# RWKV's chunked scan over chunks of 64 tokens in place of 32, with one more doubling level within a chunk

## The chip, the cores and the metric

The kernel runs on one core of one Trainium2 chip, as one program. The metric is the device time of an execution in microseconds (us). Engines are named as in the profile: PE is TensorE's matrix multiply and PEld its weight load, DVE is VectorE, ACT is ScalarE, POOL is GpSimd, SP is SyncE, which issues most transfers.

## The reference

Two small networks run one behind the other on 256 tokens of width 1024, all in float32. The first has two layers of feed-forward halves around a Fourier mixer and a retention mixer. The second has two layers; each projects its input, runs three mixers side by side (RWKV-7, compressed and windowed attention, sliding-window attention), merges them, and ends in a mixture of 16384 small experts. The change touches only the RWKV mixer, which has 8 heads of width 64. Its core is a recurrence over tokens:

```python
def step(state, inp):
    r_t, w_t, k_t, v_t, kk_t, a_t = inp
    sa = jnp.einsum('bhij,bhj->bhi', state, -kk_t)
    state = (state * w_t[:, :, None, :] + sa[..., None] * (kk_t * a_t)[:, :, None, :]
             + v_t[..., None] * k_t[:, :, None, :])
    return state, jnp.einsum('bhij,bhj->bhi', state, r_t)
```

A group norm per head, a bonus term and a gate follow.

## The kernel before, in words

The program is a list of stages. Each stage has a method for each engine, and each engine runs its stages' methods in turn; the order of the work on an engine is thus written out by hand, and semaphores (`wait_ge`, `then_inc`) tie the engines together. Weights come as blocks of 1 MB into a ring of four (`load_block`, issued by SyncE as blocks are used up). For most products ScalarE rounds a block (L232), GpSimd takes the rest (L260), and TensorE makes three products of it (L244 to L246).

In each layer of the second network the order of stages is: norm, `ProjectIn`, `Attention`, `Rwkv`, `Merge`, and then projection and experts. `Attention` begins with the preparation of RWKV's operands (`prepare_pe`, `prepare_act`, `prepare_dve`, `prepare_pool`); on VectorE `prepare_dve` stands ahead of all of the attention's own work. It takes the running sum of the log decay within each chunk by doubling: for shifts 1, 2, 4, 8, 16 a copy (L1947) and a shifted addition (L1948) between two buffers, each with the chunk as the innermost dimension. Exponentials (L1884 to L1887) and products with them (L1970 to L1976, GpSimd's L2118 to L2124) give the decayed operands A, R, b, k and the ones decayed to the end of the chunk.

The `Rwkv` stage goes over two tiles of 128 tokens (t = 0, 1), all heads at a time. Per tile:

- TensorE transposes four operands (L1773), and makes the 128x128 matrices of key products (L1784); VectorE masks them to the lower triangle within each chunk (L2023).
- The inverse of (1 + lower triangle) is built by doubling, in `LEVELS` = 5 levels: from blocks of 1 to blocks of 32. A level takes, for two groups of four heads: a mask of the level (L2033), the product ct d (L1795), a copy to SBUF by ScalarE (L1912), two more products (L1812, L1813) and the subtraction from d and dt by VectorE (L2054, L2055). Level 0 needs only L1795, L2045 and L2046. The last level updates dt alone (L1813, L2055).
- Three products with the inverse (L1817, L1820, L1826), each kept by ScalarE (L1920, L1923, L1925), give w1 and w2.
- The scan goes over the tile's four chunks of 32 tokens. TensorE: w1 times state (L1842), state times R (L1845), the update from this chunk's 32 rows (L1848), then the next chunk's keys and values, also from 32 rows (`keys_values`, L1834). VectorE: decay the state (L2073), add w2 (L2075), add keys and values (L2080), add the update (L2084). The next L1842 waits for L2084.
- The output of the whole tile within its chunks (L1856, L1857), kept by ScalarE (L1931) and VectorE (L2091).

In tile t = 1 the group norm of tile 0 is placed between the levels. TensorE: `sums(0)` after level 0's products, `squares(0)` after level 2's, `bonus(0)` after level 3's (all L1752). VectorE: `centre(0)` behind level 1 (L1992), `spread(0)` behind level 3 (L1997), `finish(0)` behind level 4 (L2004 to L2013: a reciprocal, a product, four scalings, a product, a sum, a product). ScalarE: a square (L1897) and a square root (L1901). The tests that place them name the level by its number:

```python
                if t:
                    if lv == 1:
                        centre(0)
                    if lv == 3:
                        spread(0)
                    if lv == 4:
                        finish(0)
            dve.wait_ge(s["w2_kept"].sem, s["w2_kept"].at(t + 1))
```

In t = 1, once w2 is kept, ScalarE and GpSimd begin to round and split the attention's outputs and the `Merge` stage's first weights (L2174, L232, L2194, L260) beside the scan. After the second tile come its own group norm and the first products of `Merge`.

Of the kernel before, what the change touches and what calls it, by code (L numbers as in the profile page):

```python
# [37 lines left out]
DH = 64  # L38
GN_EPS = 64e-5
HEADS = 8  # L40
CH = 32
NCH = N // CH
CMP_LEN, CMP_STRIDE = 32, 16
NCMP = N // CMP_STRIDE - CMP_LEN // CMP_STRIDE + 1
NEG = -1e30
# [47 lines left out]
class Share:  # L93
# [3 lines left out]
    def at(self, k):  # L97

        return self.base + k
# [1100 lines left out]
B_OC = B_OB + 4 * N  # L1200
B_OA = B_OC + 4 * N
B_CST2 = B_OA + 4 * N
NCST2 = 2 * P + 5 * P + 2 * 16
B_BIAS = 23328
assert B_CST2 + NCST2 <= B_BIAS
B_WORK = B_BIAS + 16 * N
# [126 lines left out]
class Attention(Stage):  # L1333
# [14 lines left out]
    def __init__(self, chip, layer, tables):  # L1348
        super().__init__(chip)
        at, sig = chip.at, chip.signals  # L1350
        self.layer, self.tables = layer, tables
        self.p = at(B_P, 56, N)
        self.o = {self.WIN: at(B_OB, 4, N), self.SWA: at(B_OC, 4, N)}
        self.bias = at(B_BIAS, 16, N)
        self.cmask = at(B_CST2 + 7 * P, 2, 16)

        self.r = at(W_R, CMP_LEN, 2, 2, NCMP)
        n = B_U
        self.hid_rows = at(n, 2 * P)
        n += 2 * P  # L1360
        self.hid = at(n, 4, 2 * NCMP)
        n += 4 * 2 * NCMP
        self.kcm, self.vcm = at(n, 16), at(n + 16, P)
        n += 16 + P
        assert n + self.BUFS * 8 * 4 <= W_PEND
        self.stat = at(n, self.BUFS, 8, 4)
        self.sc = at(B_WORK, self.BUFS, 4, N)
        n = B_WORK + self.BUFS * 4 * N
        self.pt = at(n, 5, 4, P)
        self.pts = at(n + 20 * P, 2, 4, P)  # L1370
        u = len(self.units)
        self.blocks_ready = sig("cmp_blocks_ready", 1)
        self.hidden = sig("cmp_hidden", 1)
        self.hidden_turned = sig("cmp_hidden_turned", 1)
        self.hidden_kept = sig("cmp_hidden_kept", 1)
        self.compressed = sig("cmp_done", 1)
        self.cmp_kept = sig("cmp_kept", 1)
        self.scored = sig("scored", u)
        self.biased = sig("attn_biased", u)
        self.shifted = sig("shifted", u)  # L1380
        self.exped = sig("exped", u)
        self.scale_ready = sig("attn_scale_ready", u)
        self.weighted = sig("weighted", u)
        self.turned = sig("turned", u)
        self.turned_kept = sig("attn_turned_kept", u)
        self.summed = sig("summed", u // 2)
        self.sum_kept = sig("sum_kept", u // 2)
# [256 lines left out]
class Rwkv(Stage):  # L1644
# [7 lines left out]

    LEVELS = 5

    def __init__(self, chip, layer):
        super().__init__(chip)
# [86 lines left out]
    def pe(self, pe):  # L1745
# [21 lines left out]
        for t in range(NT):  # L1767
# [66 lines left out]
                    mm(ps[:, c % 2, i * P:(i + 1) * P], self.tok[rows_, 2, i, :], self.tok[rows_, 3, i, :], start=True, stop=True)  # L1834

            keys_values(0)
            for c in range(4):
                n = 4 * t + c
                rows_ = slice(c * CH, (c + 1) * CH)
                pe.wait_ge(s["s_kept"].sem, s["s_kept"].at(n + 1))  # L1840
                for i in range(4):
                    last = mm(ps[:, 4, i * P:(i + 1) * P], self.w1[:, i, :], self.state[:, i, :], start=True, stop=True)  # L1842
                last.then_inc(s["sa_done"].sem, 1)
                for i in range(4):
                    mm(ps[:, 5, i * P + c * CH:i * P + (c + 1) * CH], self.state[:, i, :], self.R[:, i, n * CH:(n + 1) * CH], start=True, stop=True)  # L1845
                pe.wait_ge(s["sa_kept"].sem, s["sa_kept"].at(n + 1))
                for i in range(4):
                    last = mm(ps[:, 2 + c % 2, i * P:(i + 1) * P], self.tok[rows_, 1, i, :], self.sa[rows_, i, :],  # L1848
                              start=True, stop=True)
                last.then_inc(s["s_done"].sem, 1)  # L1850
                if c < 3:
                    keys_values(c + 1)
            for e in range(2):
                for i in range(4):
# [83 lines left out]
    def prepare_dve(self, dve, link):  # L1938
        ps, z, s, v = self.chip.ps, self.z, self.s, self.nc.vector
        col = lambda name, i: columns(self.chip.vec, name, self.layer, 4)[:, i:i + 1]  # L1940
        two = lambda bank: ps[:, bank:bank + 2, :].rearrange("p b (i n) -> p (b i) n", n=N)
        dve.wait_ge(s["sig_w"].sem, s["sig_w"].at(1))
        c = [x.rearrange("p i (c n) -> p (i c) n", n=CH) for x in self.c]
        link(v.tensor_scalar(self.c[0], self.c[0], -math.exp(-0.5), None, ALU.mult))
        for n in range(5):
            of, to, d = c[n % 2], c[1 - n % 2], 1 << n
            v.tensor_copy(to[:, :, 0:d], of[:, :, 0:d])  # L1947
            last = v.tensor_tensor(to[:, :, d:CH], of[:, :, d:CH], of[:, :, 0:CH - d], ALU.add)  # L1948
            if n < 4:
                link(last)  # L1950
        last.then_inc(s["c_ready"].sem, 1)
        dve.wait_ge(s["c_ready"].sem, s["c_ready"].at(1))
        e2 = self.e[2].rearrange("p i (c n) -> p (i c) n", n=CH)
        v.tensor_tensor(e2, c[1][:, :, CH - 1:CH].broadcast_to([P, 4 * NCH, CH]), c[1], ALU.subtract).then_inc(s["end_in"].sem, 1)
        dve.wait_ge(s["sig_a"].sem, s["sig_a"].at(1))
        t3 = self.t3
        for i in range(4):
            last = v.tensor_scalar(t3[:, i, :], self.a[:, i, :], 1.0, col("k_a", i), ALU.subtract, ALU.mult)
        link(last)
        k = z[:, T_K:T_K + 4, :]  # L1960
        link(v.scalar_tensor_tensor(k, t3, 1.0, k, ALU.add, ALU.mult))
        v.tensor_tensor(self.a, self.a, self.kk, ALU.mult).then_inc(s["ak_ready"].sem, 1)
        dve.wait_ge(s["ak_ready"].sem, s["ak_ready"].at(1))
        dve.wait_ge(s["exps"].sem, s["exps"].at(1))
        dve.wait_ge(s["end_exp"].sem, s["end_exp"].at(1))
        e_in, e_inv, e_end = self.e
        split = lambda x: x.rearrange("p i (c n) -> p i c n", n=CH)
        for i in range(4):
            A, kk, e = (x[:, i, :].rearrange("p (c n) -> p c n", n=CH) for x in (self.A, self.kk, e_in))
            v.tensor_tensor(A[:, :, 1:CH], kk[:, :, 1:CH], e[:, :, 0:CH - 1], ALU.mult)  # L1970
            v.tensor_copy(A[:, :, 0:1], kk[:, :, 0:1])
        v.tensor_copy(self.pend, split(e_in)[:, :, :, CH - 1])
        v.tensor_tensor(self.b, self.a, e_inv, ALU.mult).then_inc(s["ab_ready"].sem, 1)
        dve.wait_ge(s["rk_raw"].sem, s["rk_raw"].at(1))
        v.tensor_tensor(self.R, self.R, e_in, ALU.mult)
        link(v.tensor_tensor(self.k, self.k, e_inv, ALU.mult))  # L1976
        dve.wait_ge(s["hats_ready"].sem, s["hats_ready"].at(1))

    def dve(self, dve, link):
# [35 lines left out]
        for t in range(NT):  # L2015
# [47 lines left out]
                    if lv == 4:  # L2063
                        finish(0)
            dve.wait_ge(s["w2_kept"].sem, s["w2_kept"].at(t + 1))
            for c_ in range(4):
                n = 4 * t + c_
                rows_ = slice(c_ * CH, (c_ + 1) * CH)
                halves = [slice(e * DH, (e + 1) * DH) for e in range(2)]
                decayed = [self.gn[0][half, :, 0:DH] for half in halves]  # L2070
                ends = [ps[half, :, :].rearrange("p b (i n) -> p b i n", n=P)[:, :, :, half] for half in halves]
                for e, half in enumerate(halves):
                    v.tensor_tensor(decayed[e], self.state[half, :, half], self.pend[half, :, n:n + 1].broadcast_to([DH, 4, DH]), ALU.mult)  # L2073
                dve.wait_ge(s["sa_done"].sem, s["sa_done"].at(n + 1))
                last = v.tensor_tensor(self.sa[rows_].rearrange("p i n -> p (i n)"), ps[rows_, 4, :],  # L2075
                                       self.w2[rows_].rearrange("p i n -> p (i n)"), ALU.add)
                last.then_inc(s["sa_kept"].sem, 1)
                dve.wait_ge(s["sa_kept"].sem, s["sa_kept"].at(n + 1))
                for e in range(2):
                    last = v.tensor_tensor(decayed[e], decayed[e], ends[e][:, c_ % 2], ALU.add)  # L2080
                link(last)
                dve.wait_ge(s["s_done"].sem, s["s_done"].at(n + 1))
                for e, half in enumerate(halves):
                    last = v.tensor_tensor(self.state[half, :, half], decayed[e], ends[e][:, 2 + c_ % 2], ALU.add)  # L2084
                last.then_inc(s["s_kept"].sem, 1)
                dve.wait_ge(s["s_kept"].sem, s["s_kept"].at(n + 2))
# [710 lines left out]
def second_constants():  # L2797
# [3 lines left out]
    s, t = p[:, None], p[None, :]  # L2801
    same = s // CH == t // CH
    parts = [same & (s <= t), same & (s < t)]
    for n in (1, 2, 4, 8, 16):
        parts.append((s // (2 * n) == t // (2 * n)) & (s % (2 * n) < n) & (t % (2 * n) >= n))
    end = np.arange(16) * CMP_STRIDE + CMP_LEN - 1
    seen = [np.where(end[None, :] <= (p + k * P)[:, None], 0.0, NEG) for k in range(NT)]
# [267 lines left out]
```

## Time and profile before

| | us |
|---|---|
| median of 3 runs | 4928.53 |
| lowest and highest | 4918.61, 4930.82 |
| the profiled execution: span from its first to its last instruction | 4928.1 |
| busy: PE, PEld | 4534.2, 4089.3 |
| busy: DVE, ACT, POOL | 1550.8, 1764.8, 2802.4 |

The profile is of one execution, and its span stands for that execution's own time: what lies around the span is not listed apart. It is 0.4 us below the median. Busy time is the time in which an engine works on instructions; TensorE's instructions overlap, so a busy TensorE is not one at its peak. The granted clock (PEclk) is the share of 2.4 GHz that TensorE was given in a stretch; it has two levels, 1.00 (2.4 GHz) and 0.50 (1.2 GHz), and a value between them is a mean over a stretch with both. In the trace one float32 product appears as two records.

### The profile page before, as it was taken

What the parts mean: (1) busy time and instruction counts of PE and PEld (TensorE: products, weight loads), DVE (VectorE), ACT (ScalarE), POOL (GpSimd) and SP (SyncE); (2) the same over time, 40 slices, a digit from 0 to 9 for tenths busy, and PEclk for the clock granted to TensorE, in tenths of its full rate; (3) what the DMA queues carried; (4) which work ended last, traced back from release to release, by engine and by line L of the source; (5) the groups of instructions that cost most, each with busy time, mean ns of one, the idle gap of its engine ahead of it and who ended that gap; (6) DMA issues with size and microseconds to landing.
All of it is one profiled execution on the core that took longest, in us unless ns stands there. A gap on an engine that the chain in (4) does not pass through costs nothing.

```text
span 4928.1 us, 72992 instructions
## 1 busy us (share of the span) xinstructions
PE 4534.2 (92%) x30090; PEld 4089.3 (83%) x30090; DVE 1550.8 (31%) x3001; ACT 1764.8 (36%) x2766; POOL 2802.4 (57%) x1354
## 2 busy tenths in 40 slices
PE   8999999999999898998867999999998866999999
PEld 5777777787878798967856999999977866999999
DVE  2211211121023331444577111112444668111112
ACT  3223322232233343441233444444441233444444
POOL 3443333444445376830467888887840467888887
PEclk9999999999999999978788999999987888999999
DMA  6624364222223144420130454545430130545554
GB/s 253 245 89 94 113 238 179 94 94 94 93 96 119 69 171 158 171 95 1 52 112 18 180 186 179 184 182 192 167 115 1 52 112 1 186 180 181 185 179 153
DMA packets 94372, 648.51 MB, mean 132 GB/s; under 512 B 9824, under 2 KB 16224, under 8 KB 16608
## 3 DMA queue, kind: packets, MB, share of 16 engines
q1 hardware_dynamic: 87120, 633.21, 35.2%
q10 hardware_dynamic: 7056, 12.49, 1.1%
q8 instruction: 147, 2.41, 0.2%
q14 instruction: 49, 0.40, 0.0%
HBM read 641.47 MB, written 4.19 MB: 131 GB/s over the span
## 4 chain that ended last, share of the span: by engine, by line
PE 85%; DVE 11%; ACT 2%; issue 1%; POOL 1%; DMA 1%; SPq 0%; DVEq 0%; ACTq 0%; POOLq 0%
PE ps L244 23%; PE ps L245 23%; PE ps L246 23%; PE ps L2551 3%; PE ps L399 1%; PE ps L1442 1%; PE ps L1473 1%; DVE arena L2108 1%; PE ps L1795 1%; POOL ring_rest L260 1%; PE ps L1842 1%; PE ps L1005 1%; DMA arena<-in_mod_weights 1%; PE ps L1454 1%; PE ps L1848 1%
## 5 line engine op out<-in xcount | busy, mean ns | idle before, releaser
L260 POOL TENSOR_TENSOR ring_rest<-ring,rounded 128x1024 fp32r<-128x1024 f32 x1032 | 2508.4, 2452 | 1594.1 <-ACT rounded L232 1324.9
L244 PE MATMUL ps<-part,rounded 128*128 128x256 f32 (+1 forms) x5760 | 1839.0, 319 | 82.0 <-DVE part L2216 22.4
L245 PE MATMUL ps<-part,rounded 128*128 128x256 f32 (+1 forms) x5760 | 1827.2, 317 | 0.0
L246 PE MATMUL ps<-part,ring_rest 128*128 128x256 f32 (+1 forms) x5760 | 1825.7, 317 | 0.0
L244 PEld LDWEIGHTS ps<-part,rounded 128*128 128x128 f32 x5760 | 1111.7, 193 | 184.7 <-issue 27.5
L246 PEld LDWEIGHTS ps<-part,ring_rest 128*128 128x128 f32 x5760 | 1111.0, 193 | 69.1
L245 PEld LDWEIGHTS ps<-part,rounded 128*128 128x128 f32 x5760 | 1112.1, 193 | 66.9
L232 ACT ACTIVATE rounded<-ring 128x1024 fp32r<-128x1024 f32 x528 | 528.4, 1050 | 739.2 <-PE ps L246 731.3
L2673 ACT ACTIVATE rounded<-ring 128x1024 fp32r<-128x1024 f32 x504 | 531.4, 1054 | 376.3 <-DMA ring<-in_weights 369.2
L244 PE MATMUL ps<-x_parts,rounded 128*128 128x256 f32 x2304 | 654.9, 284 | 4.8 <-DVE x_parts L577 3.4
L245 PE MATMUL ps<-x_parts,rounded 128*128 128x256 f32 x2304 | 653.3, 284 | 0.0
L246 PE MATMUL ps<-x_parts,ring_rest 128*128 128x256 f32 x2304 | 653.3, 284 | 0.0
L244 PEld LDWEIGHTS ps<-x_parts,rounded 128*128 128x128 f32 x2304 | 443.7, 193 | 5.6 <-DVE x_parts L577 3.8
L245 PEld LDWEIGHTS ps<-x_parts,rounded 128*128 128x128 f32 x2304 | 443.8, 193 | 0.0
L246 PEld LDWEIGHTS ps<-x_parts,ring_rest 128*128 128x128 f32 x2304 | 443.6, 193 | 0.0
L2703 DVE TENSOR_TENSOR ps<-ps,arena 128x256 f32<-128x256 f32 x256 | 160.1, 625 | 677.0 <-ACT ps L2652 677.0
L2706 DVE TENSOR_TENSOR part<-ps,part 128x256 fp32r<-128x256 f32 x256 | 108.8, 425 | 523.0 <-ACT part L2658 523.0
L677 ACT ACTIVATE arena<-ps 128x512 f32<-128x512 f32 (+1 forms) x88 | 47.9, 544 | 617.8 <-PE ps L246 617.8
L2652 ACT ACTIVATE ps<-ps 128x256 f32<-128x256 f32 x256 | 94.2, 368 | 410.6 <-PE ps L246 410.6
L691 DVE TENSOR_TENSOR part<-ps,arena 128x512 f32<-128x512 f32 (+1 forms) x88 | 55.0, 625 | 556.9 <-ACT arena L677 556.9
L763 DVE SCALAR_TENSOR_TENSOR x<-ps,mods,x 128x256 f32<-128x256 f32 x80 | 35.8, 480 | 506.9 <-PE ps L246 506.9
L2194 POOL TENSOR_TENSOR part<-arena,part 128x1024 fp32r<-128x1024 f32 x6 | 14.2, 2369 | 290.8 <-ACT part L2174 290.8
(333 smaller groups left out, 4275.1 us busy)
## 6 DMA issues: line engine op xcount, KB each, us to landing
ring<-in_weights SPq DMA_DIRECT2D x528, 1024.0 KB, 4.8
arena<-in_mod_weights SPq DMA_DIRECT2D x72, 1024.0 KB, 7.8
arena<-bias_scratch ACTq DMA_DIRECT2D x2, 2048.0 KB, 9.1
bias_scratch<-arena ACTq DMA_DIRECT2D x1, 3072.0 KB, 32.2
x<-in_x SPq DMA_DIRECT2D x1, 2048.0 KB, 9.7
arena<-in_keys ACTq DMA_DIRECT2D x2, 1024.0 KB, 4.7
arena<-in_cst SPq DMA_DIRECT2D x1, 1216.0 KB, 28.2
arena<-in_expo ACTq DMA_DIRECT2D x1, 1024.0 KB, 4.9
```

The lines of the kernel that those rows point to most:

```text
L232: self.nc.scalar.activation(c.rounded[:, s % ROUNDED, half], c.ring[:, slot, half], ACT.Copy)\
L244: mm(out, w[0], a[0], start=start, stop=False)
L245: mm(out, w[0], a[1], start=False, stop=False)
L246: return mm(out, w[1], a[0], start=False, stop=stop)
L260: eng.tensor_tensor(c.ring_rest[:, slot, half], c.ring[:, slot, half], c.rounded[:, (self.s0 + r) % ROUNDED, half].bitcast(F32), ALU.subtr ...
L399: last = mm(c.ps[g * self.TILE:(g + 1) * self.TILE, self.BANK + n % 2, 0:width], self.cond[:, k, :], w[:, at:at + width], start=k == 0, st ...
L691: v.tensor_tensor(self.h[:, j, :], self.chip.ps[:, 2 * (j % 2) + 1, 0:self.t], self.silu[:, j % 2, :], ALU.mult)\
L2551: last = self.nc.tensor.matmul(self.chip.ps[:, n % self.BANKS, i * P:(i + 1) * P], self.hot[:, n % self.BUFS, 0, i], self.hot[:, n % self. ...
L2652: copy(self.hidden(r), c.ps[:, r % 2, 0:N], ACT.Gelu).then_inc(self.gelu_ready.sem, 1)
L2673: self.nc.scalar.activation(c.rounded[:, (self.s0 + r) % ROUNDED, half], c.ring[:, f % RING, half], ACT.Copy)\
L2703: v.tensor_tensor(gelu, gelu, self.gates[:, :, bass.ds(b, 1)].rearrange("p t a -> p (t a)"), ALU.mult)\
L2706: v.tensor_tensor(self.parts[1][:, r % 2, :], gelu, self.parts[0].bitcast(F32)[:, r % 2, :], ALU.subtract)\
```

## The change

A chunk gets 64 tokens, so a tile has two chunks (`CPT`) and the whole sequence four. The doubling within a chunk gets a sixth level, from blocks of 32 to blocks of 64, with a mask of its own in the constants, and the running sum gets a sixth shift. For the running sum to end in the same buffer, its first scaling writes to the other one. The placement of `centre`, `spread` and `finish` by level number is not touched.

```diff
-CH = 32
+CH = 64
 NCH = N // CH
+CPT = P // CH
+LEVELS = 6
+assert 1 << LEVELS == CH
...
-NCST2 = 2 * P + 5 * P + 2 * 16
+NCST2 = 2 * P + LEVELS * P + 2 * 16
...
-        self.cmask = at(B_CST2 + 7 * P, 2, 16)
+        self.cmask = at(B_CST2 + (2 + LEVELS) * P, 2, 16)
...
-    LEVELS = 5
+    LEVELS = LEVELS
...
-            for c in range(4):
-                n = 4 * t + c
+            for c in range(CPT):
+                n = CPT * t + c
...
-                if c < 3:
+                if c < CPT - 1:
                     keys_values(c + 1)
...
-        link(v.tensor_scalar(self.c[0], self.c[0], -math.exp(-0.5), None, ALU.mult))
-        for n in range(5):
-            of, to, d = c[n % 2], c[1 - n % 2], 1 << n
+        first = (LEVELS + 1) % 2
+        link(v.tensor_scalar(self.c[first], self.c[0], -math.exp(-0.5), None, ALU.mult))
+        for n in range(LEVELS):
+            of, to, d = c[(first + n) % 2], c[(first + n + 1) % 2], 1 << n
             v.tensor_copy(to[:, :, 0:d], of[:, :, 0:d])
             last = v.tensor_tensor(to[:, :, d:CH], of[:, :, d:CH], of[:, :, 0:CH - d], ALU.add)
-            if n < 4:
+            if n < LEVELS - 1:
                 link(last)
...
-            for c_ in range(4):
-                n = 4 * t + c_
+            for c_ in range(CPT):
+                n = CPT * t + c_
...
-    for n in (1, 2, 4, 8, 16):
+    for n in (1 << i for i in range(LEVELS)):
         parts.append((s // (2 * n) == t // (2 * n)) & (s % (2 * n) < n) & (t % (2 * n) >= n))
```

## Rows read from the trace of the kernel before

**Rows 1.** The page: busy time by engine, and the chain that ended last by engine.

```profile
PE 4534.2 (92%) x30090; PEld 4089.3 (83%) x30090; DVE 1550.8 (31%) x3001; ACT 1764.8 (36%) x2766; POOL 2802.4 (57%) x1354
...
PE 85%; DVE 11%; ACT 2%; issue 1%; POOL 1%; DMA 1%; SPq 0%; DVEq 0%; ACTq 0%; POOLq 0%
```

**Rows 2.** Windows, RWKV tile t = 0: length, busy by engine, granted clock, DMA share, GB/s.

```profile
2235.00:2322.00 87.00, 75.33 (x494) 71.18 (x496) 42.08 (x75) 12.46 (x22) 0.00 (x0) 0.78 0.00 1
```

**Rows 3.** Chain of waits in time, one chunk step: start, us, what.

```profile
2287.06 1.36 PE ps L1848 x5
2289.07 1.02 PE ps L1834 x5
```

**Rows 4.** Timeline of chunk steps, t = 0: start, us, engine, line, operation.

```profile
2283.44 2.08 PE L1842 MATMUL ps<-arena 128*128 128x128 f32 x8
...
2285.31 1.75 PE L1845 MATMUL ps<-arena 128*128 128x32 f32 x8
2285.55 0.68 DVE L2075 TENSOR_TENSOR arena<-ps,arena 32x512 f32<-32x512 f32 x1 [3.27 <-PE ps L1842]
...
2289.17 0.85 DVE L2084 TENSOR_TENSOR arena<-arena,ps 64x256 f32<-64x256 f32 x2 [2.05 <-PE ps L1848]
...
2290.08 2.07 PE L1842 MATMUL ps<-arena 128*128 128x128 f32 x8
...
2306.89 2.07 PE L1848 MATMUL ps<-arena 32*128 32x128 f32 x8
```

**Rows 5.** Timeline of doubling levels, t = 0, second head group and last level.

```profile
2263.23 1.13 PE L1795 MATMUL ps<-arena 128*128 128x128 f32 x8 [0.71 <-DVE arena L2055]
...
2269.54 1.13 PE L1795 MATMUL ps<-arena 128*128 128x128 f32 x8 [0.71 <-DVE arena L2055]
...
2271.67 0.69 DVE L2055 TENSOR_TENSOR arena<-arena,ps 128x512 f32<-128x512 f32 x1 [2.28 <-PE ps L1813]
```

**Rows 6.** Windows around levels, scan, output products and attention (columns as rows 2).

```profile
2243.00:2247.00 4.00, 2.43 (x12) 2.46 (x13) 2.40 (x5) 0.00 (x0) 0.00 (x0) 0.71 0.00 0
2247.00:2251.00 4.00, 2.79 (x17) 2.34 (x17) 3.93 (x7) 0.60 (x1) 0.00 (x0) 0.87 0.00 0
...
2263.00:2267.00 4.00, 3.77 (x34) 3.80 (x35) 1.59 (x4) 0.75 (x2) 0.00 (x0) 1.00 0.00 0
...
2283.00:2287.00 4.00, 4.00 (x20) 3.71 (x19) 1.40 (x3) 0.00 (x0) 0.00 (x0) 0.50 0.00 0
...
2183.00:2189.00 6.00, 6.00 (x16) 4.18 (x16) 2.86 (x5) 2.12 (x10) 0.28 (x1) 0.50 0.00 0
...
2309.00:2314.60 5.60, 5.60 (x32) 5.44 (x32) 0.84 (x2) 0.00 (x0) 0.00 (x0) 0.65 0.00 0
```

**Rows 7.** Timeline of TensorE: attention scores, first level, w1 and w2 products.

```profile
2181.74 3.78 PE L1442 MATMUL ps<-arena 64*128 64x256 f32 x8
...
2244.57 3.65 PE L1795 MATMUL ps<-arena 128*128 128x128 f32 x16 [3.16 <-DVE arena L2033]
...
2273.36 1.83 PE L1817 MATMUL ps<-arena 128*128 128x128 f32 x14 [0.85 <-DVE arena L2055]
...
2277.84 2.85 PE L1826 MATMUL ps<-arena 128*128 128x64 f32 x16 [0.69 <-ACT arena L1923]
```

**Rows 8.** Timeline of VectorE, t = 1: finish(0) and the first chunk steps.

```profile
2358.61 3.35 DVE L2004 RECIPROCAL arena<-arena 128x512 f32<-128x512 f32 x1
...
2365.32 0.69 DVE L2013 TENSOR_TENSOR arena<-arena 128x512 f32<-128x512 f32 x1
2366.54 0.85 DVE L2073 TENSOR_TENSOR arena<-arena 64x256 f32<-64x256 f32 x2 [0.53 <-ACT arena L1925]
...
2375.24 4.35 DVE L2073 TENSOR_TENSOR arena<-arena 64x256 f32<-64x256 f32 x2
```

**Rows 9.** Chain of waits in time, the running sum in prepare_dve.

```profile
2126.01 0.20 DVE arena L1947
...
2127.34 0.20 DVE arena L1947
```

## The prediction

> **What bounds the kernel now.** First the page's busy shares and its chain of waits: TensorE is busy 92% of the span and is 85% of the chain that ended last [rows 1]. The change touches only the RWKV part of the two layers of the second network: two token tiles (t = 0 and t = 1, 128 tokens each) in each layer, four tiles in all, 87 us for the first and about as much for each of the others [rows 2]. So a few per cent of the span are in play, and what a step is worth has to be read from the timeline.
>
> Second the chain through one chunk step of the scan (t = 0). It stays on TensorE: the products with w1 (L1842), those with the state (L1845), those that give the new state (L1848), the next chunk's keys and values (L1834), then the next step [rows 3]. The timeline gives the pitch: the step's first product starts at 2283.44 and again at 2290.08, thus 6.64 us [rows 4]. VectorE's work (L2075, L2084) lies just beside it: L2084 runs from 2289.17 to 2290.02, 0.06 us before the next L1842, so both engines bound the step nearly equally [rows 4].
>
> Third the doubling levels: the second head group's L1795 starts at 2263.23 and again at 2269.54, a pitch of 6.31 us, at a granted clock of 1.00 (2.4 GHz) [rows 5, 6]. The scan runs at 0.50 (1.2 GHz) although TensorE is busy 4.00 of each 4.00 us [rows 6]. That is the heart of the trade: a level costs nearly what a chunk step costs.
>
> **What the change does, part by part.** *Fewer chunk steps.* Two steps go from each tile, whole ones, since the last stays the last: 2 x 6.64 = 13.28 us less per tile. The two that stay get larger operands. L1848 and L1834 contract over 64 rows in place of 32: 8 records of 32 rows take 2.07 us (L1848) and 8 of 128 rows 2.08 (L1842) [rows 4], so 64 rows cost the same. L1845 gets 64 columns for 32; 8 records take 1.75 us with 32 columns and 2.08 us with 128 (L1842) [rows 4], so at most 0.33 us more per step, 2.6 us over the 8 steps left; I take nothing, because 16 records of 64 columns (L1826) take 2.85 us, less for each than the 1.75 for 8 [rows 4, 7]. L2075 reads 64 partitions for 32 with the same 512 elements in each: 0.68 us, while L2055 with 128 partitions takes 0.69 [rows 4, 5]; nothing. The two pend columns fewer per tile are a copy of a few elements.
>
> The 4 L1848 products and the next chunk's 4 L1834 products fill the chain from 2287.06 to 2290.08, 3.0 us, where 16 records at 0.22 us (8 L1845 from 2285.31 to 2287.06) would need 3.5 [rows 3, 4]: they overlap a little at their border because they sit on different row strips. With 64 rows they still do (0:64 and 64:128). If they did not: 0.5 us per whole step, 2.0 us over four tiles. The Trainium skill speaks against this change here (TensorEngine Tiling, When to Use Tiling): a contraction of 32 allows 4x row tiling, one of 64 only 2x. By that rule the removed concurrency would raise each step's price; the rows show that the products of one chunk, all on one strip, were never concurrent, so the sum leaves it out.
>
> *One more level.* + 6.31 us per tile, read at the full clock. Its masks (L2033) go one level ahead and are in that pitch. It is inserted before the last one, which is shorter on VectorE in old and new alike.
>
> *Where finish(0) stands.* In t = 1 VectorE does the previous tile's group norm: centre after level 1, spread after 3, finish after level 4. Level 4 was the last, so finish(0) ran beside TensorE's w1, x2 and w2 products: from 2358.61 to 2366.01, 7.40 us, and VectorE had nothing to do until 2366.54 anyway [rows 8]. Its cost was nothing, and its cover was the wait for w2. The diff leaves the test at level 4, now the last but one; finish(0) stands ahead of the last level's L2055. At t = 0 VectorE is idle for 2.28 us, until 2271.67, between the L2055 of these two levels [rows 5]. So 7.40 - 2.28 = 5.1 us stick out on the path, once per layer. Queued behind it on VectorE are the last L2055s; w1, x2 and w2 on TensorE wait for them, and then ScalarE and the scan. The root that finish needs is there: ScalarE's square root follows its level-4 copies and its table load, and TensorE's bonus sums come at level 3, so neither adds a wait. The pause on TensorE grows from 0.85 us [rows 7] to 6.0.
>
> *The clock behind that pause.* After the 3.16 us pause ahead of the first level, L1795 ran its 16 records in 3.65 us [rows 7]; the clock was 0.71 and 0.87 in those two stretches of 4 us, which is 2.3 and 1.0 us at half clock [rows 6]. L1817 has 16 records of the same kind and took 1.83 for 14 at full clock [rows 7]. So 3.3 us at half clock cost 1.7 us; if the low clock holds on for L1820 it is as much again, and 0.5 for L1826, partly slow already: + 1.7 to + 3.9. I take 2.0 per layer, nearest to the one episode that rows 6 show.
>
> *The prefix sum in prepare_dve.* The list of shifts becomes 1 to 32 over 16 groups of 64, in place of 1 to 16 over 32 groups of 32. A copy of n x d elements and an addition of the rest: shifts 2 to 32 of the new have the sizes of 1 to 16 of the old, and the new first one (copy of 16, sum of 1008) costs about what the old first did, from 2126.01 to 2127.34: + 1.3 us. This lies on the chain [rows 9], so + 1.3 per layer. The other exponentials and products keep their sizes.
>
> *The constants* grow by 128 columns (one more mask) in a load issued long before: nothing.
>
> *POOL's splitting of weights in t = 1* makes a copy group of VectorE (L2073) last 4.35 us for 0.85 in the second chunk step [rows 8]. It starts after w2 as before, two steps remain and so does this stall: nothing either way.
>
> **Sum.** t = 0: - 13.3 + 6.3 = - 7.0. t = 1: - 13.3 + 6.3 + 5.1 + 2.0 = + 0.1. Prefix sum + 1.3. One layer - 5.6 us, two layers - 11.2 us. Against the profiled execution's span of 4928.1 us this is 4916.9; that execution is 0.4 us below the median of the runs shown (4928.53), so 4917.3, and I predict 4917 us. About 0.3%, 15 us, is what a measurement of this kernel can tell from no change; the three runs lie 12 us apart. The forecast is just within it.
>
> **The rivals.** *Full clock in the scan* (chance 0.12). The scan's matmuls fill a quarter of the array's rows (L1848, L1834) or of the columns (L1845), and the change doubles each. For: the full 128x128 work of L1856 and L1857 that follows the scan in t = 0 brings the clock back (0.65 from 2309 to 2314.6) [rows 6]. Against: the attention's 64-row, 256-column products stand at 0.50 too (L1442, and the stretch from 2183 to 2189) [rows 6, 7], and those are as full as the new ones. Then a step becomes, L1842 and L1848 at half their 2.08 and 2.07, L2075 0.7, L2084 0.9 and an estimated 0.3 of hand-overs = 4.0 in place of 6.6. Two steps per tile, 2.6 each, and about 2 for L1856 and L1857, which now are half slow: 7 per tile, 28 in all: 4889 us; half of it if only two tiles get there, 4903. The Trainium skill (TensorE: Matmul & The Clock Gate, Part 1) has it that sustained activity of TensorE releases the throttle. By that rule the scan of before, busy 4.00 of 4.00 us, would run at full clock; the trace disagrees, at 0.50, so the rule alone gives this rival no more.
>
> *The late finish is hidden after all* (0.10). If the pause does not cost the 2.0, and finish overlaps more than I see, both layers get up to 2 x 7.1 = 14.2 back: 4903 us. Against: VectorE executes in program order, and 7.40 us do not fit in 2.28.
>
> *The trade turns round* (0.10): the added level runs at the low clock. Its place is the last level of each tile; its price: 16 L1795 records and 32 of L1812/L1813 at 0.22 us are 10.5 us in place of 6.3. For it: the first level of t = 0 began at 0.71 after a pause [rows 6], and in t = 1 group-norm work stands between the levels. In all four tiles, with finish and the 3.9 of its pause: t = 0 - 2.8, t = 1 + 6.2, prefix + 1.3: + 4.7 per layer, + 9 in all, 4937 us, slower than before. It decides where the added level exceeds its 6.3 by 2.8 us on average over the four tiles, since that is the forecast's 11.2. Against: at t = 0 the levels from the third on stand at 1.00. To be slower by more than 15 us, other levels would have to slow down too.
>
> *Forecast* (0.68): 4917, own range 4909 to 4926 (the bounds of L1845 and the clock terms, and up to 1.2 us per tile for where in L1856/L1857 the clock comes back).
>
> **Chances and range.** Faster by over 0.3% (below 4913.7): the full clock 0.12, most of the hidden finish 0.07, and 0.13 from the forecast's lower end: 0.32. Slower by over 0.3%: 0.03. Within: 0.65. The range 4902 to 4927 leaves out the full clock in all tiles and most of the turned trade.
>
> **What would show it.** Right: two L1842 pitches of 6.6 us per tile fewer; L1795 for six levels, with a pitch of 6.3 us at t = 0; the RWKV tile of t = 0 shorter by 7 us and that of t = 1 by nearly nothing; in t = 1, L2004 ahead of the last two L2055, and TensorE waiting about 6 us ahead of L1817 for L2055; L1817 above 3 us; six pairs of L1947/L1948, 1.3 us more. Wrong: a granted clock of 1.00 between L1834 and L1848, a step longer than 7 us at t = 0, or L1817 following the last level within 1 us in t = 1.

## The result and the profile after

| | before | after | ratio, 95% interval |
|---|---|---|---|
| first measurement, 4 runs each: median us | 4923.84 | 4895.21 | 0.9947 [0.9930, 0.9963] |
| second measurement, 9 and 5 runs | 4926.55 | 4894.61 | 0.9933 [0.9920, 0.9947] |

The change makes the kernel 29 to 32 us faster. I had said 11 us, with a range that ended at 4902, so the direction held and the size did not. The first profile of after is of an execution of 4900.47 us, the slowest of its four; a second profile (called `again` below) is of one of 4894.61 us, the median of its five.

The page of the first profile of after, busy time and chain by engine:

```profile
PE 4489.2 (92%) x30026; PEld 4049.4 (83%) x30026; DVE 1542.7 (31%) x2973; ACT 1770.5 (36%) x2774; POOL 2804.4 (57%) x1354
...
PE 84%; DVE 11%; ACT 2%; issue 1%; POOL 1%; DMA 1%; SPq 0%; DVEq 0%; ACTq 0%; POOLq 0%
```

Next to [rows 1], TensorE's busy time fell by 45 us. The trade explains some 30 of them: eight steps of 6.6 us, all busy, against four levels of 48 records at 0.12 us. The other 15 us are time that the trade does not account for; since a busy TensorE takes longer at the lower clock, they point to the granted clock, which the stretches below show.

The scan of tile t = 0 in layer 0 (timeline of after):

```profile
2282.38 2.07 PE L1845 MATMUL ps<-arena 128*128 128x128 f32 x8
2284.24 1.81 PE L1848 MATMUL ps<-arena 128*128 128x64 f32 x8
...
2289.07 2.08 PE L1845 MATMUL ps<-arena 128*128 128x128 f32 x8
...
2292.68 2.07 PE L1851 MATMUL ps<-arena 64*128 64x128 f32 x8
```

Line numbers are 3 higher than before at this place. Against [rows 4]: the pitch is 2289.07 - 2282.38 = 6.69 us (6.64 before), L1848 with 64 columns takes 1.81 us (1.75 with 32), and L1851 with 64 rows 2.07 (the same as with 32). Larger operands cost next to nothing, as costed.

The late finish(0) in tile t = 1 (timeline of `again`, VectorE, then TensorE):

```profile
2345.16 0.68 DVE L2059 TENSOR_TENSOR arena<-arena,ps 128x512 f32<-128x512 f32 x1
2345.88 3.35 DVE L2008 RECIPROCAL arena<-arena 128x512 f32<-128x512 f32 x1
...
2352.59 0.69 DVE L2017 TENSOR_TENSOR arena<-arena 128x512 f32<-128x512 f32 x1
2353.20 1.40 DVE L2059 TENSOR_TENSOR arena<-arena,ps 128x512 f32<-128x512 f32 x2
...
2354.66 3.78 PE L1820 MATMUL ps<-arena 128*128 128x128 f32 x16 [5.70 <-DVE arena L2059]
```

(Here the line numbers are 4 higher than before.) The reciprocal starts right behind level 4's L2059, the last level's two L2059 wait until 2353.20, and TensorE's pause ahead of L1820 is 5.70 us in place of 0.85 [rows 7]. L1820 then runs at the low clock, 3.78 us.

So where did the rest come from? The two profiles, cut at the same instructions (the running sum's scaling, the first attention scores, the first transpose, the first w1 product, the first keys-and-values product, the first output product, finish(1)'s last product); all in us, `again` less before:

| stretch | layer 0 | layer 1 | predicted, per layer |
|---|---|---|---|
| preparation with the running sum | + 1.3 | + 1.3 | + 1.3 |
| attention | - 9.2 | - 7.2 | 0 |
| t = 0: levels | + 6.8 | + 5.7 | + 6.3 |
| t = 0: w1 to w2 | - 0.9 | - 0.2 | 0 |
| t = 0: scan | - 13.2 | - 13.2 | - 13.3 |
| t = 0: output | + 0.7 | 0.0 | 0 |
| t = 1: levels with finish(0) | + 11.9 | + 11.2 | + 11.4 |
| t = 1: w1 to w2 | + 1.9 | + 1.7 | + 2.0 |
| t = 1: scan | - 13.4 | - 13.4 | - 13.3 |
| t = 1: output, group norm, first of Merge | - 3.0 | - 2.9 | 0 |
| sum | - 17.0 | - 17.1 | - 5.6 |

Every term that I costed is within 0.7 us, and the small stretches without a term within 0.9. What is missing is one stretch that the change does not touch: the attention, 16.4 us in the two layers, and 5.9 us behind the last scan. The attention of both kernels (windows from the first score to the first transpose; length, busy by engine with instruction counts, granted clock, DMA share, GB/s). Before, layer 0 and layer 1:

```profile
2151.45:2235.68 84.23, 78.30 (x260) 48.95 (x260) 34.18 (x88) 43.33 (x156) 18.74 (x16) 0.69 0.00 1
3641.38:3722.79 81.41, 75.47 (x260) 47.08 (x261) 34.56 (x88) 43.04 (x156) 18.74 (x16) 0.71 0.00 1
```

`again`:

```profile
2151.29:2226.33 75.04, 69.10 (x260) 44.01 (x261) 34.57 (x88) 43.00 (x156) 18.74 (x16) 0.77 0.00 1
3624.12:3698.34 74.22, 68.29 (x260) 44.05 (x260) 34.59 (x88) 42.88 (x156) 18.74 (x16) 0.78 0.00 1
```

The same 260 records, the same work of VectorE, ScalarE and GpSimd, but TensorE's clock is 0.77 where it was 0.69. The timelines of layer 0 show where they part. Before:

```profile
2151.45 7.19 PE L1442 MATMUL ps<-arena 64*128 64x15 f32 x32 [6.19 <-DVE arena L1561]
...
2168.49 5.78 PE L1473 MATMUL ps<-arena 15*128 15x512 f32 x6
2174.21 2.07 PE L1442 MATMUL ps<-arena 64*128 64x128 f32 x8
```

`again`:

```profile
2151.29 7.19 PE L1445 MATMUL ps<-arena 64*128 64x15 f32 x32 [7.50 <-DVE arena L1564]
...
2168.34 5.78 PE L1476 MATMUL ps<-arena 15*128 15x512 f32 x6
2174.05 1.55 PE L1445 MATMUL ps<-arena 64*128 64x128 f32 x8
```

For 23 us both run in step at half clock. Then the new kernel's scores shorten to 1.55 us, while the old one's stay at 2.07: its clock comes back only about 22 us later, near the end of the L1473 that start at 2191.25. The one thing that differs ahead of this stretch is TensorE's pause, 7.50 us for 6.19: the 1.3 us of the longer running sum.

Layer 1 parts in another way. There the clock comes back 22 to 23 us behind the first score in both kernels, but before it falls again 44 us behind it, for 14 us. Before, then `again`:

```profile
3664.60:3685.00 20.40, 19.42 (x97) 12.93 (x97) 15.39 (x35) 16.77 (x64) 7.02 (x6) 1.00 0.01 1
3685.10:3698.60 13.50, 13.50 (x30) 7.52 (x29) 4.58 (x10) 4.61 (x15) 3.10 (x3) 0.50 0.00 1
...
3646.10:3683.50 37.40, 33.51 (x153) 21.08 (x152) 23.71 (x53) 28.38 (x99) 12.48 (x10) 1.00 0.00 1
```

The 3 us behind the last scan of each layer are a matter of the clock too: the same 170 records, at 0.82 before and at 0.94 in `again` (layer 0). In layer 1 of the first profile of after, with the same chunks of 64, they were at 0.84 and took 26.26 us:

```profile
2395.63:2422.30 26.67, 24.49 (x170) 24.30 (x170) 10.14 (x14) 5.49 (x7) 5.35 (x3) 0.82 0.15 45
2380.16:2403.84 23.68, 21.51 (x170) 21.32 (x170) 10.13 (x14) 5.49 (x7) 5.35 (x3) 0.94 0.16 51
```

### The profile page after: what moved, and what is told of

It reads as the page before. It is cut to its first block, busy times and chain, and to the rows that moved or that the text cites. A ratio compares the mean times of both kernels' runs of the same rounds, so it can differ in the third digit from the quotient of the medians.

```text
span 4898.7 us, 72852 instructions
## 1 busy us (share of the span) xinstructions
PE 4489.2 (92%) x30026; PEld 4049.4 (83%) x30026; DVE 1542.7 (31%) x2973; ACT 1770.5 (36%) x2774; POOL 2804.4 (57%) x1354
## 4 chain that ended last, share of the span: by engine, by line
PE 84%; DVE 11%; ACT 2%; issue 1%; POOL 1%; DMA 1%; SPq 0%; DVEq 0%; ACTq 0%; POOLq 0%
PE ps L247 24%; PE ps L248 23%; PE ps L249 23%; PE ps L2555 3%; PE ps L402 1%; PE ps L1445 1%; PE ps L1476 1%; DVE arena L2112 1%; PE ps L1798 1%; POOL ring_rest L263 1%; PE ps L1008 1%; DMA arena<-in_mod_weights 1%; DVE arena L2444 1%; DVE arena L2437 1%; DVE arena L2474 1%
```

## The experiments

Two theories stood against each other. **Alignment**: how much of the attention runs at the full clock depends on the moment of its first product, and the 1.3 us more ahead of it moved that moment to a better place. **Clock by size** (my rival; the texts below also say clock theory and, later, occupancy theory): products with more rows and columns lift the clock. **Price** names the plain sum of steps.

### The changed kernel again

No edit.

> The changed kernel once more, for a second profile. Price theory (the steps cost what the timeline says, and what goes beyond 11 us is where the granted clock happens to rise and fall in one execution): the difference to before shrinks towards - 11 to - 18 us over more runs, and the stretch from the running sum to the first transposes, - 7.9 us in layer 0 and + 4.3 in layer 1 in the first profile, comes out otherwise. Clock theory (the 64-row and 64-column products lift the granted clock): again - 26 to - 30 us, and the scans of layer 1, 14.1 and 15.8 us shorter than before in the first profile, are again shorter than the 13.3 of two steps.

Measured: 4894.61 us, ratio 0.9933 [0.9920, 0.9947]. The gain did not shrink to the 11 to 18 us of the price theory, so it is not the chance of one execution. But it is no gain of the scans either: in this profile all four stand at 0.50, for example

```profile
2278.03:2292.30 14.27, 14.27 (x65) 13.30 (x65) 5.52 (x12) 0.00 (x0) 0.00 (x0) 0.50 0.00 1
```

In the first profile the attention of layer 1 took 84.38 us at 0.69 and a scan of layer 1 ran at 0.80 (13.22 us), so either can fall otherwise in one execution. That execution was 6 us slower than this one. Ahead of that attention the two executions of the same program differ by 0.2 us: the granted clock fell 5.38 us ahead of the first score in `again`, and 5.58 us in the first profile (windows up to the fall, and from it to the first score):

```profile
3616.72:3618.72 2.00, 0.71 (x10) 0.50 (x9) 1.51 (x1) 0.78 (x1) 2.00 (x2) 1.00 0.86 352
3618.76:3624.12 5.36, 0.00 (x0) 0.00 (x1) 5.24 (x5) 0.00 (x0) 3.54 (x2) 0.50 0.56 234
...
3619.10:3621.10 2.00, 0.82 (x11) 0.61 (x10) 1.31 (x1) 0.89 (x1) 2.00 (x2) 1.00 0.72 299
3621.14:3626.70 5.56, 0.00 (x0) 0.00 (x0) 5.45 (x5) 0.00 (x0) 3.75 (x2) 0.50 0.59 239
```

The first has 74.22 us of attention behind it, the second 84.38.

### finish(0) behind the last level

```diff
-                    if lv == 4:
+                    if lv == self.LEVELS - 1:
                         finish(0)
```

> The changed kernel with finish(0) back behind the last level. The late finish is priced at 5.1 us of waiting and 2.0 of clock per layer, so price theory expects 14 us less than the changed kernel (11 to 18), L1820 (w1) following the last level after 0.85 us instead of 5.70 us. Rival, that the pause is made good elsewhere (the clock comes back later in the scan all the same): under 5 us less.

Measured: 4882.76 us, 0.9906 [0.9891, 0.9921] of before; 11.9 us less than `again` in the same measurement. Between the two profiles the levels of t = 1 in layer 0 take 48.88 in place of 53.75 us (4.9, costed at 5.1), and w1 to w2 7.54 in place of 9.88 (2.3, costed at 2.0):

```profile
2352.56 2.05 PE L1820 MATMUL ps<-arena 128*128 128x128 f32 x16 [0.85 <-DVE arena L2059]
```

The price of the late finish is near the 14 us predicted; the rival, that it is made good elsewhere, is out.

### A level alone

```diff
-    LEVELS = 5
+    LEVELS = 6
...
-                    if lv == 4:
+                    if lv == self.LEVELS - 1:
                         finish(0)
```

(With the mask of the sixth level added to the constants; chunks stay at 32.)

> The kernel before (chunks of 32) with a sixth level whose mask leaves nothing to add, and finish(0) behind that last level. It gives the price of a level alone: price theory 4 x 6.3 = + 25 us over before, at most + 31 with slow stretches; if the level runs at the low clock, 4 x 10.5 = + 42.

Measured: 4948.14 us, 1.0044 [1.0030, 1.0057], + 21.6 us for four levels. A level at the low clock (+ 42) is out. The useful part is another: the preparation is that of before, and so is the attention, to 0.01 us:

```profile
2149.18:2233.41 84.23, 78.30 (x261) 49.00 (x261) 34.17 (x88) 43.33 (x156) 18.73 (x16) 0.69 0.00 1
3649.35:3730.75 81.40, 75.47 (x260) 47.10 (x261) 34.58 (x88) 43.02 (x156) 18.74 (x16) 0.71 0.00 1
```

The output stretch of t = 1 fell to 23.7 us in layer 0 and 24.4 in layer 1 (26.7 and 26.5 before), with chunks of 32. So that 3 us does not come from the size of the chunks either.

### Chunks of 64 without the sixth level

```diff
-    LEVELS = LEVELS
+    LEVELS = 5
```

> The changed kernel without its sixth level (5 levels; the doubling from 32 to 64 is left out, so finish(0) is behind the last level again). It gives the chunk halving alone with the longer running sum: price theory - 8 x 6.64 + 2.6 = - 50.5 us against before. Clock theory: - 60 us or more, since the larger products of the scan and what follows would run at the full clock part of the time.

Measured: 4853.35 us, 0.9861 [0.9845, 0.9877], - 73.2 us. This kernel leaves out the doubling from 32 to 64. Its gain goes beyond the - 50.5 of the price theory, and by this number the clock theory seemed right. The profile says otherwise: the scans are at 0.50, 0.53, 0.50 and 0.50, 14.3 to 15.6 us, just what the price theory has, and the attention is at 75.04 and 74.17 us. The number fitted the wrong cause; 16 of the 23 us beyond the price stand in the attention.

### The delay alone, in the kernel before

```diff
-        for n in range(5):
+        for n in (0, 0, 1, 2, 3, 4):
             of, to, d = c[n % 2], c[1 - n % 2], 1 << n
```

> The kernel before with its first shift of the running sum done twice in each layer (same result, 1.33 us more on VectorE in prepare_dve, nothing else). Alignment theory (which stretch of the attention runs at full clock depends on how long TensorE waits ahead of it, so that 1.3 us more there bring the clock back about 20 us earlier): faster than before by about 2 x 7 = 14 us, the attention 75 and 74 us long in place of 84.2 and 81.4. Rival (the larger chunks do it, or the shorter attention has another cause): slower by 2 to 3 us.

Measured: 4914.85 us against 4923.06 (11 and 15 runs), 0.9988 [0.9978, 0.9998]: 8 us faster, with 1.33 us of useless work added per layer. The median of before is lower here than in the measurement ahead (4926.55), and its runs go from 4911 to 4931. The attention is that of the changed kernel:

```profile
2152.90:2227.93 75.03, 69.09 (x261) 43.95 (x261) 34.58 (x88) 42.99 (x156) 18.74 (x16) 0.77 0.00 1
3632.64:3706.79 74.15, 68.21 (x261) 44.00 (x261) 34.56 (x88) 42.87 (x156) 18.73 (x16) 0.78 0.00 1
```

The rival (+ 2 to 3 us) is out, and the attention's two lengths, without any larger chunk, settle what moved it. In time the run gave less than the 14 us expected: 8, with an interval from 1 to 11 us, and this profile is of the fastest of its eleven executions (4909.60).

### The delay taken out of the changed kernel

```diff
-        link(v.tensor_scalar(self.c[first], self.c[0], -math.exp(-0.5), None, ALU.mult))
-        for n in range(LEVELS):
+        link(v.tensor_scalar(self.c[0], self.c[0], -math.exp(-0.5), None, ALU.mult))
+        for n in range(1, LEVELS):
```

> The changed kernel without the shift by one in the running sum (5 pairs of copy and addition in place of 6, so 1.3 us less per layer; what that shift adds is left out, so the decays differ). Alignment theory: slower than the changed kernel by about 14 us, near 4910, the attention back at 84 and 81 us. Rival: faster by 2 to 3 us, near 4892.

This kernel leaves out the shift by one, its time and what it adds to the sum. Measured: 4904.41 us, 0.9961 [0.9946, 0.9975]; the changed kernel had 4894.61 and 0.9933 in the measurement ahead, so this is 10 us slower with less work. The attention is back at the values of before:

```profile
2151.03:2235.26 84.23, 78.30 (x260) 48.93 (x261) 34.18 (x88) 43.33 (x156) 18.74 (x16) 0.69 0.00 1
3627.43:3708.76 81.33, 75.39 (x260) 47.03 (x261) 34.57 (x88) 43.02 (x156) 18.73 (x16) 0.71 0.00 1
```

So the delay decides over the attention in both kernels, and the size of the chunks in neither.

### More delay

```diff
-        for n in range(5):
+        for n in (0, 0, 0, 1, 2, 3, 4):
```

> The kernel before with the first shift done three times in each layer, 2.66 us more ahead of the attention (same result). It asks how far the alignment reaches. If a longer pause is all that counts, the attention stays at 75 and 74 us, near 4917. If it is where the pause falls against the clock's own decisions, it may be at 84 and 81 again: near 4929.

> As before_plus2 with the first shift done four times, 4.0 us more. Same two outcomes: near 4920 if the longer pause is all that counts, 4926 to 4935 if the attention falls back. Rival to both: the time follows the added work alone, + 8 us over before, whatever the attention does.

`before_plus3` has one more 0 in the list. Measured: 4918.95 us, 0.9989 [0.9979, 0.9998], and 4917.05 us, 0.9987 [0.9977, 0.9996], beside 4925.82 for before (25 runs). The attention takes 75.18 and 75.22 us with 2.66 us more, but 76.83 and 81.12 with 4.0 us:

```profile
3637.82:3718.94 81.12, 75.19 (x261) 47.06 (x261) 34.55 (x88) 42.91 (x156) 18.73 (x16) 0.71 0.00 1
```

A longer pause is thus not better as such: in layer 1 the third step loses what the first gave. Work does not add up to time here either, since 1.3, 2.7 and 4.0 us more all end below before. I had put `before_plus3` at 4920 or above; it came out lower, with gains in other stretches (the output of t = 1 in layer 1: 24.0 for 26.5 us).

### Wider and fuller products in the scan

Does the size of the scan's products matter to the clock at all? `wide_finish_last`, on top of finish(0) behind the last level:

```diff
-                    mm(ps[:, 5, i * P + c * CH:i * P + (c + 1) * CH], self.state[:, i, :], self.R[:, i, n * CH:(n + 1) * CH], start=True, stop=True)
+                    mm(ps[:, 5, i * P + c * CH:(i + 1) * P], self.state[:, i, :], self.R[:, i, n * CH:(t + 1) * P], start=True, stop=True)
```

> finish(0) behind the last level, and the products of the state with R (L1848) cover all columns of the tile from the chunk's first on, 128 for chunk 0 in place of 64; the later chunk writes its own again, so the result stays. Occupancy theory (the scan stands at 0.50 because its matmuls fill too little of the array): the scan's clock rises above 0.50 in some scans and the time falls below 4883 by 3 to 10 us. Price theory: same as finish_last within 2 us, since 128 columns cost 0.1 us more than 64.

Measured: 4877.05 us, 0.9904 [0.9889, 0.9919]. Three of the four scans, at 0.72, 0.76, 0.75 and 0.72, are shorter than 14.3 and 15.6 us:

```profile
2278.67:2289.74 11.07, 10.61 (x65) 9.76 (x65) 5.53 (x12) 0.00 (x0) 0.00 (x0) 0.72 0.01 1
2352.18:2365.49 13.31, 10.74 (x64) 9.84 (x64) 7.98 (x12) 5.53 (x6) 12.44 (x6) 0.76 0.00 0
3747.09:3757.87 10.78, 10.32 (x65) 9.58 (x65) 5.52 (x12) 0.00 (x0) 0.00 (x0) 0.75 0.01 2
3818.25:3833.85 15.60, 11.49 (x64) 10.49 (x65) 9.67 (x13) 5.52 (x6) 14.27 (x6) 0.72 0.00 0
```

The fourth is at 0.72 too, but there VectorE's slow L2077 (5.00 us for two) beside GpSimd sets the length. The kernel's median is 5.7 us below that of `finish_last`, in another measurement; by their ratios to before the two are the same (0.9904 and 0.9906), so the total does not show the 3 to 10 us expected, and only the scans do. The layer-1 attention of this profile was a slow one (84.34 us). `full_rows`:

```diff
-                    mm(ps[:, c % 2, i * P:(i + 1) * P], self.tok[rows_, 2, i, :], self.tok[rows_, 3, i, :], start=True, stop=True)
+                    mm(ps[:, c % 2, i * P:(i + 1) * P], self.tok[:, 2, i, :], self.tok[:, 3, i, :], start=True, stop=True)
...
-                    last = mm(ps[:, 2 + c % 2, i * P:(i + 1) * P], self.tok[rows_, 1, i, :], self.sa[rows_, i, :],
+                    last = mm(ps[:, 2 + c % 2, i * P:(i + 1) * P], self.tok[:, 1, i, :], self.sa[:, i, :],
```

> The changed kernel with all 128 rows in the state update and in the keys and values, in place of the chunk's 64 (this adds the other chunk's terms, so the output is another one). Every product of the scan but L1848 then fills the whole array. Occupancy theory: the scans go from 0.50 towards 1.00, 14.3 and 15.6 us shrink to 9 to 11, and the four together give 15 to 20 us. If the clock does not look at rows: no difference to the changed kernel within 3 us.

Measured: 4865.19 us, 0.9883 [0.9866, 0.9900], 29 us below the changed kernel's 4894.61, in another measurement. It adds the other chunk's terms, so its result is another one. Its scan of t = 1 in layer 0:

```profile
2351.87:2361.87 10.00, 7.84 (x65) 7.44 (x65) 7.98 (x12) 5.53 (x6) 9.12 (x4) 1.00 0.00 0
```

Here the clock theory holds: the same count of products, with more rows filled, gets the full clock. The other three scans are at 0.73 to 0.76, and the four together take 43.8 us, 16 less than in `again` (15 to 20 expected). The profile is of the slowest of its four executions (4875.36). `wide_before` is the widening in the kernel before:

> The kernel before (chunks of 32) with its products of the state with R (L1845) widened to all columns from the chunk's first to the tile's end: 128, 96, 64 and 32 columns in place of 32 each, same result. Occupancy theory: the scans of before, 0.50 throughout, rise above 0.50 as they did with chunks of 64 (0.72 to 0.76), and the time falls by 5 to 20 us. If the 32-row products hold the clock down by themselves: within 3 us of before.

Measured: 4921.88 us, 0.9995 [0.9985, 1.0005]. Its scans are at 0.50, 0.65, 0.64 and 0.50: something rises, but with 32-row products beside it only in part, and the total does not tell it from before. The expected 5 to 20 us was too much, and the fall of 4 us lies within the noise.

### The fastest version that leaves nothing out

`wide_finish_last` with the first shift done twice (`for n in (0, *range(LEVELS))`).

> wide_finish_last with one shift of the running sum done twice (2.66 us more than before ahead of the attention, 1.33 more than wide_finish_last). Work-follows-time: 4880, 2.7 us more than wide_finish_last. Alignment theory: not within 2 us of that, since the attention of layer 1 in wide_finish_last's profile was at 84 us and that of layer 0 at 75.

Measured: 4871.65 us, 0.9891 [0.9875, 0.9908], 54 us under before and 5.4 under `wide_finish_last` in another measurement, with 1.3 us more work per layer, and 8 under the 4880 that the added work alone would give. Both attentions are fast, 74.43 and 75.18 us, which in `wide_finish_last` only one was. (`full_rows` and `chunks_only` are faster and compute something else.)

## Why the prediction was wrong

**The step that failed** is the prefix sum: "so + 1.3 per layer". Its duration is right to 0.03 us, 27.45 in place of 26.17 us for the preparation. What I put at nothing is what it does to the stretch behind it: by delaying the attention it moves the first score against the clock's course, worth - 9.2 and - 7.2 us, 16.4 of the 22 us by which the forecast was off. The 5.9 us behind the last scans, the same work at 0.94 in place of 0.82, are the rest; I had allowed 1.2 us per tile there. I had priced such an effect of a longer pause behind finish(0), as a loss, and nowhere as a gain. My sum had a clock term at the pause that grew by 5 us and none at the one that grew by 1.3. That this one came out as a gain is luck: 1.3 us more gave 7 to 9 us here, but with 0.2 us of difference the same program has the slow attention in layer 1.

**The chunk steps** (- 13.3 per tile): right, - 13.2 and - 13.4. The added columns cost 0.06 us of at most 0.33. My ground for taking nothing was a poor one: the L1826 that I compared with ran partly at the full clock, L1845 at the low one.

**The level** (+ 6.3): right in the profiles, + 6.8 and + 5.7 at t = 0.

**finish(0)** (+ 5.1 and 2.0 of clock): right, 4.9 and 2.3 by `finish_last`; it costs 12 of the 14 us per program.

**The sum without the alignment** came out right, in part by luck. The profiles of `again` and `before_plus1`, which share the preparation and the attention's alignment, differ by 15.0 us in span; my terms less the prefix sum give 13.8. But two terms that I did not have cancel in it: per layer the scan of t = 1 gives 11.0 us in place of 13.3, since it was already shorter in `before_plus1` (26.67 us at 0.53, for 28.97 at 0.50 in before), and the stretch behind it gives 2.7 that I had at nothing. And the medians differ by 20 us, in two measurements: the profile of `before_plus1` is of an execution 5 us below its median, that of `again` is its median. What makes the other executions of `before_plus1` slower is open.

**The full clock in the scan** (rival, 0.12, 4889 us) came nearest in time and was wrong in cause for this change: seven of the eight scans of the two profiles are at 0.54 or below, the eighth at 0.80. The mechanism exists, as `full_rows` and `wide_finish_last` show, but 64 rows and columns reach it only now and then. Against the rival I had put the attention's stretch at 0.50 [rows 6] as a fixed property of its products. It was the very stretch that moved: from 2183 to 2189, where I read 0.50, `again` has the same products at the full clock. Had I asked what decides when the low clock ends there, the missing term would have been in view.

**Not there**: the hidden finish and the added level at the low clock; TensorE's pause of 5.70 us and the 21.6 us of `level_only` exclude both.

**A reading that was off**: the tiles of t = 1 are not about 87 us long but 105; no term of the sum rests on it.

**Open**: what sets the clock behind the last scan (0.94 and 0.91 also in `level_only`, with chunks of 32, but not in `before_plus1`, where that stretch took 26.4 us); what moves the first score by 0.2 us between two executions; and the spread of before's own runs, 4910 to 4931. That the fast ones among them have a fast attention is a guess, since no profile of one was taken.

## What to carry to other kernels

When a change moves the start of a dense stretch that begins at the low clock, by however little, its length can change by more than all the costed steps, as here (16 us against 11); look for the points at which the clock falls and comes back around it, and put the lengths seen for such a stretch in the range as a gain and as a loss. A number that fits a theory is not yet that theory: - 73 us fitted the clock in the scan, and the stretches by clock put it elsewhere. Level numbers written out (`lv == 4`) should move with the loop that they count, here 12 us.

## What the runs showed of the hardware

The clock's course repeats closely between executions and programs with the same timing ahead. In all fourteen profiles the length of the attention, the same products each time, goes with one distance, the time from the clock's last fall to the first score:

| fall ahead of the first score, us | attention, us | profiles |
|---|---|---|
| 4.1 to 4.3 | 81.3 to 81.4 | layer 1 of before, `level_only`, `after_short`, `wide_before` |
| 5.4 to 5.5 | 74.2 | layer 1 of `again`, `finish_last`, `chunks_only`, `before_plus1`; layer 0 of `full_rows` |
| 5.6 | 84.3 to 84.4 | layer 1 of after (first profile), `wide_finish_last`, `full_rows` |
| 5.8 | 84.2 | layer 0 of before, `level_only`, `after_short`, `wide_before` |
| 6.8 to 6.9 | 75.2 | both layers of `before_plus2`; layer 1 of `wide_finish_plus1` |
| 7.1 | 75.0 to 75.1 | layer 0 of after, `again`, `finish_last`, `chunks_only`, `wide_finish_last`, `before_plus1` |
| 8.1 | 81.1 | layer 1 of `before_plus3` |
| 8.5 | 74.4 | layer 0 of `wide_finish_plus1` |
| 9.7 | 76.8 | layer 0 of `before_plus3` |

Between 5.5 and 5.6 the length jumps by 10 us. More distance is not better as such: what 1.3 us more are worth hangs on where one starts.

Being busy was not enough to bring the clock back. The scan of t = 0 in before is busy for all of its 27.4 us and stays at 0.50, with 32 rows in two of its four kinds of product and 32 columns in a third; with chunks of 64 it is at 0.50 to 0.54 in most profiles, at 0.80 in two scans of t = 1 (after, `after_short`). From there, with 128 columns in one kind of product it reaches 0.72 to 0.76 in all eight scans of two profiles, with 128 rows in two kinds 0.73 to 1.00 in the four of one. The Trainium skill (TensorE: Matmul & The Clock Gate, Part 1) speaks of how busy TensorE is; the trace agrees for the levels (1.00), not for these scans, where the rows and columns that the products fill made the difference. At the low clock, columns added to such products cost at most 0.2 us per 8 records (1.75 us with 32, 1.92 with 128), rows nothing (2.07 us with 32 and with 64), and both can pay by the clock. What fill it takes was not measured.
